# First output projection of a hybrid encoder step: from two token parts of plain tiles to a seven-product scheme over two K panels, with h through DRAM

## The reference

```
n = rmsnorm(x);  z = n @ w_in                      # q, k, v, forget gate, gates, u
att = forgetting_attention(q, k, v, logf)          # 8 heads of 128, causal, a cache of 512 for the sample
ssm = s5(u)                                        # gelu, then y * sigmoid(y @ w_glu)
mixed = concat(att * silu(ga), ssm * silu(gs))     # 2048 wide
h = x + mixed @ w_out                              # the matmul that is changed
e = rmsnorm(p @ w_pe)
h = h + e * sigmoid(h @ w_pg)
y = rmsnorm(h)
```

## Time and profile before

| | us |
|---|---|
| median of 3 runs (lowest, highest) | 2473.47 (2468.51, 2474.2) |
| the profiled execution | 2475.24 |
| its span | 2473.5 |
| TensorE busy, share | 2272.9, 92% |
| TensorE weight loads, share | 2138.9, 86% |
| VectorE busy, share | 1593.3, 64% |
| ScalarE busy, share | 781.4, 32% |
| GpSimd busy, share | 317.3, 13% |

### The profile page before, as it was taken

How to read it: one execution, slowest core, us unless ns; L and a number is a source line. 1 busy time by engine, 2 the same in 40 slices (tenths; PEclk the granted TensorE clock), 3 DMA queues, 4 the chain that set the end, 5 groups by cost and what they waited for, 6 DMA issues and landing times. The chain is left out here.

```text
span 2473.5 us, 43304 instructions
## 1 busy us (share of the span) xinstructions
PE 2272.9 (92%) x16025; PEld 2138.9 (86%) x16025; DVE 1593.3 (64%) x2934; ACT 781.4 (32%) x1651; POOL 317.3 (13%) x350
## 2 busy tenths in 40 slices
PE   3989999999899999999688877888999999999996
PEld 3989999999899999999577757886888888999996
DVE  6768766776777878884377754755445666334664
ACT  6442333333433333333465534321001113001112
POOL 0011000000112112111233314200001110001110
PEclk9999999999999999999799888998999999999998
DMA  7474444444767788774455524435445446434332
GB/s 236 143 241 113 133 130 129 146 136 136 263 196 213 216 229 229 218 222 128 167 167 172 163 68 181 149 124 175 119 114 164 121 112 200 115 107 130 107 104 97
DMA packets 399412, 390.28 MB, mean 158 GB/s; under 512 B 73896, under 2 KB 341704, under 8 KB 392800
## 3 DMA queue, kind: packets, MB, share of 16 engines
q1 hardware_dynamic: 354176, 271.50, 38.1%
q0 software_dynamic: 20704, 77.95, 9.6%
q10 hardware_dynamic: 24384, 38.87, 4.9%
HBM read 257.56 MB, written 122.01 MB: 153 GB/s over the span
## 5 line engine op out<-in xcount | busy, mean ns | idle before, releaser
L745 PE MATMUL acc<-t_act,w_hi 128*128 128x264 f32 x5376 | 889.3, 288 | 20.0 <-DVE zb L1321 8.0
L745 PEld LDWEIGHTS acc<-t_act,w_hi 128*128 128x128 f32 x5376 | 749.8, 189 | 27.2 <-issue 25.7
L745 PE MATMUL acc<-t_act,w_lo 128*128 128x264 f32 x2688 | 549.0, 286 | 0.0
L2608 PE MATMUL post_acc<-region_hi,w_post_hi 128*128 128x272 f32 (+1 forms) x1536 | 419.0, 327 | 23.7 <-DVE region_lo L2717 19.0
L745 PEld LDWEIGHTS acc<-t_act,w_lo 128*128 128x128 f32 x2688 | 418.0, 189 | 0.0
L2608 PE MATMUL post_acc<-region_hi,w_post_lo 128*128 128x272 f32 (+1 forms) x1536 | 416.1, 325 | 0.0
L2608 PE MATMUL post_acc<-region_lo,w_post_hi 128*128 128x272 f32 (+1 forms) x1536 | 415.4, 325 | 0.0
L1296 DVE TENSOR_TENSOR w_lo<-w_raw_f,w_hi 128x512 fp32r<-128x512 f32 x288 | 198.0, 687 | 164.4 <-ACT w_hi L953 164.2
L2608 PEld LDWEIGHTS post_acc<-region_hi,w_post_hi 128*128 128x128 f32 x1536 | 258.6, 189 | 49.8 <-issue 16.2
L2608 PEld LDWEIGHTS post_acc<-region_lo,w_post_hi 128*128 128x128 f32 x1536 | 259.0, 190 | 22.2
L2608 PEld LDWEIGHTS post_acc<-region_hi,w_post_lo 128*128 128x128 f32 x1536 | 257.5, 190 | 22.8
(11 more groups left out here) (381 smaller groups left out, 3249.1 us busy)
## 6 DMA issues: line engine op xcount, KB each, us to landing
w_raw_f<-in_w_in_dram SPq DMA_DIRECT2D x96, 512.0 KB, 4.0
w_raw<-in_w_out_dram SPq DMA_DIRECT2D x64, 512.0 KB, 4.7
w_raw<-in_w_pg_dram SPq DMA_DIRECT2D x64, 512.0 KB, 4.7
cT<-zb SPq DMA_DIRECT2D x24, 1056.0 KB, 4.3
zb<-cT POOLq DMA_DIRECT2D x96, 264.0 KB, 5.9
zT<-zb POOLq DMA_DIRECT2D x80, 264.0 KB, 3.5
eT<-e_out ACTq DMA_DIRECT2D x16, 528.0 KB, 3.0
t_act<-tS POOLq DMA_DIRECT2D x7, 1056.0 KB, 10.4
```

Of the source, the lines that this page charges most:

```text
L745: mm = pe.matmul(out[:, c, 0:QN], w[:, k, :], t_act[:, SIDE[r], x, k, c * QN:(c + 1) * QN], start=(opens and k == 0 and m == 0), stop=(k = ...
L2608: mm = pe.matmul(acc[b][:, c, 0:width], w[:, k, :], a[region][:, k, start:start + width], start=(k == 0 and n == 0), stop=(k == KD - 1 and ...
```

## The change

Phases 0 and 2 leave the output stage. A new stage, `stage_mix`, between the side stage and the output stage, computes h = x + mixed @ w_out by the front's seven-product scheme: two K panels, 8 passes of 256 output columns in each, 7 products a pass, 24 matmuls of 264 tokens a product. The first panel's blocks come straight from `mixT`; the combined sides of the second panel are made on the way ("rides", in passes 1 to 4) and kept in `tS`. The first panel's sums go through `cT`. The second panel's passes add x and store h to a new DRAM tensor `hT`. The output stage then has only the two w_pg parts, loads h from `hT` as it loaded `mixed` before, and has one `hi`, `lo`, `y_tok` and `g_bc` where it had two regions. Besides, head 0's q, k and v rows are loaded by the front stage, and `p_in` by the attention stage, into the top of SBUF.

The core of the diff (a line of "..." where lines are left out):

```diff
+                if p == GATES[1]:
+                    sp.wait_ge(v_used, NPB)
+                    sp.wait_ge(y_stored[(NPB - 1) % 3], 128 * len(range((NPB - 1) % 3, NPB, 3)))
+                    for i in range(4):
+                        sp.wait_ge(z_put[i], put_count(LAST_RECUR))
+                    for x, row, loaded in zip(G["first_raw"], (0, D_ATT, 2 * D_ATT), G["first_loaded"]):
+                        sp.dma_start(x[:], d["zT"][row:row + P]).then_inc(loaded, 16)
...
+            for done, n in ((q_hi_done, HEADS), (q_lo_done, HEADS), (k_hi_done, HEADS), (k_lo_done, HEADS),
+                            (k_turned, 3 * HEADS), (v_turned, 3 * HEADS)):
+                sp.wait_ge(done, n)
+            sp.dma_start(G["p_in"][:, 0:TT], d["p_prompt"][0, 0].rearrange("(i p) c -> p i c", p=P)) \
+                .then_inc(G["p_loaded"], 16)
+            sp.dma_start(G["p_in"][0:T_SAMPLE, TT], d["p_sample"][0, 0]).then_inc(G["p_loaded"], 16)
...
-            sp.dma_start(p_in[:, 0:TT], p_rows).then_inc(p_loaded, 16)
-            sp.dma_start(p_in[0:T_SAMPLE, TT], d["p_sample"][0, 0]).then_inc(p_tail_loaded, 16)
...
-            prefetch(sp, G["shared"], d["w_out"], 0)
...
-            pool.wait_ge(p_loaded, 16)
+            pool.wait_ge(p_loaded, 32)
...
+def stage_mix(nc, d, G):
...
+            sp.dma_start(plain(0), block_of(0, 0, 0)).then_inc(raw_loaded["b11"], 16)
+            sp.dma_start(zb[0][:], block_of(0, 0, 1)).then_inc(raw_loaded["b12"], 16)
+            load_w(0, 0)
+            load_w(0, 1)
+            sp.dma_start(plain(5), block_of(0, 1, 1)).then_inc(raw_loaded["b22"], 16)
+            sp.dma_start(plain(3), block_of(0, 1, 0)).then_inc(raw_loaded["b21"], 16)
+            load_w(1, 0)
+            prefetch(sp, G["shared"], d["w_pg"], 0)
+            for p in range(2 * NPM):
+                load_w(p + 1, 1)
+                if 1 <= p <= NPM:
+                    sp.wait_ge(added, p)
+                    sp.dma_start(d["cT"][p - 1], zb[(p - 1) % 2][:]).then_inc(z_stored[(p - 1) % 2], 16)
+                if p >= NPM:
+                    if p > NPM:
+                        sp.wait_ge(h_added, 4 * (p - NPM))
+                    sp.dma_start(slots(x_res), rows_of("xT", p)).then_inc(x_loaded, 16)
+                load_w(p + 2, 0)
...
+            def reload_side(s):
+
+                pool.wait_ge(sides_moved[s], RELOADED[s] - 16)
+                pool.wait_ge(prod_done, 7 * (NPM - 1) + s + 1)
+                src = {0: block_of(1, 0, 0), 3: block_of(1, 1, 0), 5: block_of(1, 1, 1)}[s] if s in (0, 3, 5) \
+                    else d["tS"][s]
+                pool.dma_start(plain(s), src).then_inc(sides_moved[s], 16)
+
+            def store_h(p):
+
+                for n, i in enumerate((0, 3, 1, 2)):
+                    pool.wait_ge(h_added, 4 * (p - NPM) + n + 1)
+                    row, tok = p % NPM * 2 * P + i // 2 * P, i % 2 * HN
+                    pool.dma_start(d["hT"][row:row + P, tok:tok + HN], zb[p % 2][:, i]).then_inc(z_put[i], 16)
+
+            def load_part(p):
+
+                b = p % 2
+                if p - 2 < NPM:
+                    pool.wait_ge(z_stored[b], 16 * (p // 2))
+                for i, _ in DONE if p > NPM + 1 else reversed(DONE):
+                    if p - 2 >= NPM:
+                        pool.wait_ge(z_put[i], PUT + mix_count(p - 2))
+                    if p > NPM:
+                        pool.wait_ge(z_got[i], GOT + mix_count(p - 1))
+                    pool.dma_start(zb[b][:, i], d["cT"][p - NPM][:, i]).then_inc(z_got[i], 16)
+
...
+            def product(p, r):
+                n, s = 7 * p + r, (7 * p + r) % RING_W
+                out = acc[:, AT["XBYXYBY"[r]]:AT["XBYXYBY"[r]] + 2]
...
+                for k in range(KQ):
+                    for m, (w, x) in enumerate(((w_hi[s], 0), (w_hi[s], 1), (w_lo[s], 0))):
+                        for c in range(2):
+                            mm = pe.matmul(out[:, c, 0:QN], w[:, k, :], t_act[:, SIDE[r], x, k, c * QN:(c + 1) * QN],
+                                           start=(opens and k == 0 and m == 0), stop=(k == KQ - 1 and m == 2),
+                                           skip_group_check=True)
+                mm.then_inc(prod_done, 1)
+
+            for p in range(2 * NPM):
+                for r in range(7):
+                    product(p, r)
...
+                    if j == 5 and NPM - 1 <= p < last:
+                        seed_x(p + 1)
+                    high(7 * p + j + RING_W - 1)
+                    for s in range(7):
+                        if 7 * p + j == 7 * (NPM - 1) + s + 3:
+                            act.wait_ge(sides_moved[s], RELOADED[s])
+                            high_side(7 + s, s)
...
+            dve.wait_ge(raw_loaded["b11"], 16)
+            dve.wait_ge(raw_loaded["b12"], 16)
+            TT_(first_side[1], zb[0][:], plain(0), ALU.subtract).then_inc(t_sub, 1)
+            low_side(0, 0)
+            sums(1)
+            low(0)
+            dve.wait_ge(raw_loaded["b22"], 16)
+            dve.wait_ge(t_sub, 1)
+            TT_(first_side[2], plain(5), first_side[1], ALU.subtract).then_inc(t_sub, 1)
+            low_side(1, 1)
+            sums(2)
+            low(1)
+            dve.wait_ge(raw_loaded["b21"], 16)
+            dve.wait_ge(t_sub, 2)
+            TT_(first_side[6], plain(3), first_side[2], ALU.subtract).then_inc(t_sub, 1)
+            low_side(2, 2)
+            low(2)
+            TT_(first_side[4], plain(5), zb[0][:], ALU.subtract).then_inc(t_sub, 1)
+            low_side(3, 3)
+            for p in range(2 * NPM):
+                for j in range(7):
+                    if p == 0 and j < 3:
+                        low_side(4 + j, 4 + j)
+                    if j == 3 and p >= NPM:
+                        u2(p)
+                    if j == 4 and p >= NPM:
+                        c11(p)
+                    if j == 5:
+                        c22(p)
+                    if j == 6:
+                        c12(p)
+                    sums(7 * p + j + RING_W)
+                    low(7 * p + j + RING_W - 1)
+                    if 1 <= p <= NPM and j == 1:
+                        add_parts(p - 1)
+                    if 1 <= p <= NRIDE and j == 2:
+                        subtract_rides(p - 1)
+                    for s in range(7):
+                        if 7 * p + j == 7 * (NPM - 1) + s + 4:
+                            low_side(7 + s, s)
+                    if p >= NPM and j >= 5:
+                        residual(p, j - 5)
+                    if p > NPM and j < 2:
+                        residual(p - 1, j + 2)
+            residual(last, 2)
+            residual(last, 3)
...
+                if part == 0:
+                    pool.dma_start(g_bc[:], d["g_final"].unsqueeze(0).to_broadcast([P, D_MODEL])) \
+                        .then_inc(g_loaded, 16)
-                pool.wait_ge(W.gemm_done, part * 2 * KD + KD)
-                pool.dma_start(g_bc[part][:], d["g_final"].unsqueeze(0).to_broadcast([P, D_MODEL])) \
-                    .then_inc(g_loaded, 16)
...
-                if part == 0:
-                    for k in range(4):
-                        high_mix(1, k)
                 sigmoid(part, KD - 1, 1, KD // 2 - 1)
                 if part == 0:
-                    for k in range(4, KD):
-                        high_mix(1, k)
+                    for k in range(KD):
+                        high_h(1, k)
...
+                if part and isinstance(m, int) and m == 0:
+                    for t in range(len(ROWS[0])):
+                        dve.wait_ge(y_stored[t], stored_count(0, t))
...
         stage_side(nc, d, G)
+        stage_mix(nc, d, G)
         stage_output(nc, d, G)
```

More of the change, by code:

```diff
@@ L57 @@
 RF = 34
+NPM, NRIDE = 8, 4
+SIDE = (0, 2, 3, 1, 4, 5, 6)
 RING_W = 4
@@ L2525, in y_store @@
             dst = d["y_sample"][0] if rows < P else y_tiles[BASE[part] // P + t]
-            eng.dma_start(dst, y_tok[part][0:rows, t]).then_inc(y_stored[t], 16)
+            eng.dma_start(dst, y_tok[0:rows, t]).then_inc(y_stored[t], 16)
         def stored_count(part, t):
@@ L2532, in _, with load @@
         def _(sp):
-            def load(phase, m, b, it):
-                part, gate = phase // 2, phase % 2 == 1
-                if phase or not isinstance(m, int) or m:
-                    W.load(sp, w_pg if gate else w_out, m * P, m + phase * KD)
-                if (gate and not isinstance(m, int)) or (not gate and isinstance(m, int) and part):
+            def load(part, m, b, it):
+                if part or not isinstance(m, int) or m:
+                    W.load(sp, w_pg, m * P, m + part * KD)
+                if part or not isinstance(m, int) or m >= 2:
                     sp.wait_ge(e_scaled, m + (part * KD - 1))
-                else:
-                    sp.wait_ge(evacuated[b], it + phase * (KD // 2))
                 sp.dma_start(side[b][:, 0:WIDTH[part]],
```

(20 more changed lines are left out.)

457 lines of the change are left out of this document (349 added, 108 removed).

## The result

The change made the kernel slower. Over nine executions of each on the same chip the changed kernel took 2479.76 us in the median (2470.56 to 2488.77), the one before 2468.51 (2462.0 to 2474.2); the ratio of their runs is 1.0042, 95% interval [1.0024, 1.0060], so by it 10.4 us (6 to 15) more (the medians lie 11.2 apart). I had forecast 4 us less, with 0.30 for slower.

The account below looks back on a forecast made before the run. TensorE, working through 92% of the span, was taken as the bound. Terms: -395.1 + 329.3 + 27.9 + 9.6 + 6.0 + 16.2 + 2.5 + 8.4 - 8.8 = -4.0, so 2473.5 became 2469.5 us; 8-in-10 range 2453 to 2490.

Parts of the forecast that it names:

- new stage, release to last matmul: The added stage_mix: products 329.3 us, first-pass loss 27.9 and panel switch 9.6.
- end of the first pass: New stage: VectorE's queue makes the first pass end 48.5 us after release, 27.9 of it loss; bounds 15.5 and 34.
- panel switch: New stage, change to the second K panel: 9.6 us lost, as in the front stage; bounds 3 and 18.
- end of the new stage: After its last matmul: copy, residual add, store issue, landing and block's end, together 6.0 us.
- w_pg stage, release to last matmul: Output stage's two w_pg parts: old phases 185.0 and 200.8 us, plus 16.2, 2.5 and 8.4.
- the loads ahead: Attention and side stage starts: loads issued a stage earlier save 3.9 and 4.9 us, together 8.8; bounds -4 and -12.
- the 2.5 for g_bc: w_pg stage's start: g_bc's 1 MB issued beside the loads of h costs 2.5 us; range 0 to 3.5.
- The pitch: New stage: products follow each other 2.94 us apart, 122.5 ns a matmul, so 112 products take 329.3 us.
- Rival (c): New stage's second panel doesn't keep TensorE's pace: 3 us lost in each of seven passes gives 2490 us; chance 0.14.
- Rival (d): Starts dearer: first-pass half clock +6, switch at 15 +5, y_tok's stores +4, giving 2485 us; chance 0.16.
- the wait for y_tok's stores: w_pg part 1: VectorE's first fill waits for stores; 0.5 us taken, bounds 0 and 6, +4 in Rival (d).
- case (a): Whole kernel: no change that can be told, 2466.1 to 2480.9 us; chance 0.38 with a rival that preloads bring nothing.

Follow-up runs that it names:

- e2: Changed kernel with the last pass's four stores of h issued by SyncE instead of GpSimd; ratio to before 1.0017, +4.2 us.
- e9: Changed kernel with one more GpSimd queue drain behind the stores of the last pass but one; ratio to before 1.0002, +0.5 us.
- e5: Kernel before with the four loads moved ahead and the front stage's last stores of z on SyncE instead of GpSimd; ratio to before 0.9949, -12.6 us.
- e6: e2 with g_bc's 1 MB broadcast issued behind the last low part of h; ratio to before 1.0009, +2.2 us.
- e7: e2 with VectorE splitting the second w_pg tile among the low parts of h, in both parts; ratio to before 0.9963, -9.1 us.
- e1: Kernel before with only the loads of q, k, v and p moved a stage ahead; ratio to before 0.9966, -8.4 us.
- e4: Changed kernel with ScalarE copying the first pass's Y seed ahead of the fourth subtraction's high side; ratio to before 1.0028, +6.9 us.

## Why the prediction was wrong

The sum's terms against what the trace of the kernel after shows, each from its own release:

| term | predicted | measured | miss |
|---|---|---|---|
| new stage, release to last matmul | 366.8 | 369.2 | +2.4 |
| of it: end of the first pass | 48.5 | 48.2 | -0.3 |
| of it: panel switch | 9.6 | 12.4 | +2.8 |
| end of the new stage | 6.0 | 12.5 | +6.5 |
| w_pg stage, release to last matmul | 412.9 | 417.8 | +4.9 |
| the loads ahead | -8.8 | -7.1 | +1.7 |

The forecasts of the two stages are the sum's own terms (329.3 + 27.9 + 9.6; and 185.0 + 200.8, the two w_pg phases before, + 16.2 + 2.5 + 8.4). Together +15.5: from the forecast -4.0 to +11.5. The two traces lie 13.6 apart, 11.5 without the front's 2.1, and the times say +10.4.

**What failed** is the step "The end of the new stage", priced at 6.0 us with "0.6 for the block's end". It measured 12.5, and 7.8 of them are a term that I had put at nothing: the drain of GpSimd's queue. I gave the step no bounds either. 0.6 us is near the drain behind a stage in which GpSimd issued eight DMAs (the output stage of before, 0.72 us); the new stage has 95. This miss alone turns -4.0 into +2.5. The front's end, the only one in the trace before at which GpSimd issues the last stores after hundreds of DMAs, had the figure. Its last store in the kernel before:

```profile
1202.61 0.54 POOL L635 DMA_DIRECT2D zT<-zb  x1
```

SyncE was released at 1213.60, 10.5 us after that issue ended, of which 3.5 are the landing and 5.5 the drain. I had taken the landing from the grouped issues and not set the last store beside the next stage's first instruction. e2, e9 and e5 show the mechanism from three sides.

**The w_pg stage** was 4.9 us dearer, half of it in each part. Tile 1 started 29.6 us after the release, not 28.5: the 2.5 for g_bc were right (e6), but GpSimd's additions now fall on VectorE's split (e7 and the rows there), which I had not counted among what moved. With the longer gap (4.6 us, 2.4 before) went a longer stretch at the lower clock, too. From the start of tile 1, the granted clock (the last column but two) after and, in a second fence, before:

```profile
2075.00:2080.00 5.00, 4.13 (x10) 3.26 (x11) 2.86 (x4) 0.00 (x0) 1.28 (x1) 0.50 1.11 347
2080.00:2085.00 5.00, 5.00 (x22) 4.04 (x21) 3.22 (x4) 0.15 (x1) 0.00 (x0) 0.82 0.44 119
```

```profile
1695.50:1700.50 5.00, 4.94 (x15) 3.90 (x16) 1.30 (x3) 0.62 (x1) 0.00 (x0) 0.66 0.92 259
1700.50:1705.50 5.00, 5.00 (x23) 4.06 (x22) 3.56 (x4) 0.00 (x0) 0.00 (x0) 1.00 0.27 73
```

0.50 is 1.2 GHz and 1.00 is 2.4 GHz; 0.50 and 0.82 in the mean of two windows of 5 us, against 0.66 and 1.00. Part 1 has the other half, 2.4 us: its first tile took 18.9 instead of 18.1, and the rest, with the same stall of 2.1 that I had forecast at 2.3, 192.7 for 15 tiles of 12.55 and that stall (190.4). No run takes this last part asunder.

**The loads ahead** were near in sum, in good part by luck, and wrong in both halves, as e1 shows (5.5 of the trace's 7.1 us lie inside the attention stage, where the sum had nothing): I had stopped at the wait that goes, k's landing, and not asked GpSimd's program, whose mask casts end 2.1 us after the release, nor what a y_raw that starts sooner does to the weights behind it. That y_raw is the cause there is not tested. Bounds of -4 to -12 held.

**What held.** The pitch: 1176 matmuls in 143.8 us of the second panel, 122.3 ns each, for a forecast of 122.5. The first pass, by the queue on VectorE; e4 shows that this queue sets all but 1.6 us of its end. That the end came within 0.3 us is luck: product 0 started at 13.9 us and not at 15.5, since the first two blocks had landed after 8.0, and the copy of the seed, which the forecast did not have, took the 1.6 us back. Rival (c), a second panel that does not keep pace: TensorE was busy for 143.80 of 143.80 us there. Rival (d) gave a time near the measured one (2485, 11.5 over before) for reasons that mostly did not come: of the first pass's clock, the switch and the wait for y_tok's stores only the switch cost more than priced, by 2.8 of the 5 us. Two slips in the rivals changed nothing: two landings of 10.4 us exceed (c)'s 14 by 6.8 a pass, so by 48 and not 40 in seven, and case (a) stands with two ranges (2466.1 to 2480.9, then 2463 to 2479).

So the mechanisms priced from rows of a like stage (pitch, switch, queue) came within 3 us, and the largest miss, 6.5 of the 15.5 us, lies where one stage hands over to the next. The seven-product scheme had 45 us of TensorE time to give and spent them and 19 more on first pass, switch, stage end and a second start.

## What to carry to other kernels

Price a new stage border from a border of the same kind: the last instruction of one stage to the first of the next, with the engine that issues the last transfer the same. If GpSimd issues many DMAs in a stage, let another engine issue the last stores, or write a drain where GpSimd idles: here 7 to 9 us at one border and 5 at another in the traces, for a few lines. And a bundle of edits is to be measured apart: here one part gave some 8 us and the other took some 19.

## What the runs showed of the hardware

- GpSimd's queue drain at the end of a block took 7.82, 7.58 and 7.50 us after 95, 92 and 91 DMAs, 0.38 after 4, 0.72 and 0.62 after 8 and 7, 0.03 after none, and one written out in mid-stage starts the count anew. It adds to the time until the last transfer has landed (side stage before: 5.34 us after 9 DMAs, the last issued when it began; DMAs of this kind landed in 5.0 there). In the front stage 218 DMAs gave 5.46 us and 214 gave 5.13: the same 0.08 for each one taken away, but not 0.08 times all of them. What resets part of the count there is open.
- Two casts and two subtractions of 128x1024 on VectorE took 3.6 us alone and 5.8 us beside two additions of GpSimd.
- A wait of 9.2 us in TensorE's list was worth 1.6 us when its releaser came sooner, since the wait behind it was nearly as late.
- The attention stage took 244.7 us at a granted clock of 0.94, 246.0 at 0.92 and 251.5 to 252.2 at 0.90, in traces of nearly the same program.
